# Two transformer blocks on one core: four first tiles instead of one go through the arriving token blocks

## The chip, the cores and the metric
The kernel runs on one core of a Trainium2 chip. The time is that of one launch in microseconds of device time. TensorE multiplies, VectorE (DVE), ScalarE (ACT) and GpSimd (POOL) work on rows of 128 partitions, SyncE (SP) issues all DMA transfers. Each engine runs its own instructions in order and waits at semaphores.

## The reference
Two blocks over 512 tokens of width 1024. Only the beginning matters here: the input norm, the first projection and the norm of the memory.

```python
h = rms_norm(x, norm_mix_g[layer])
proj = h @ w_in                                   # 2560 columns of the first mixer and 256 of q_mem
slab = token_shift(proj[..., :RWKV_COLS], mu)     # z + (z_prev - z) * mu
r, k, v, wd, ad, gd = split(slab)                 # 768 each; 64, 64, 128
log_w = -softplus(-(w0 + tanh(wd) @ w2)) - 0.5
a = sigmoid(a0 + ad @ a2);  g = sigmoid(gd) @ g2
kv = rms_norm(mem, mem_norm_g) @ w_mem_kv         # 256 memory tokens
```

The rest (a delta-rule scan over six pairs of heads, memory attention, two feed-forward parts, two kinds of local attention in the second block) is not touched.

## The kernel before, in words
The activations lie with the features in the partitions: eight blocks of 128 features by 512 tokens. (They are called token blocks here, as the functions that handle them are called `token`.) A weight unit is 128x1024. For precision every factor is split in a high and a low part (`Whi`, `Wlo`, `Hhi`, `Hlo`), and a block of a tile is three matmuls (hi·hi, lo·hi, hi·lo) of 128x512 into one PSUM bank (`mm3`, all at line 906). A tile is eight blocks, 24 matmuls. The norm's factor is applied behind the product, when the tile is evicted, so matmuls can run before the sum of squares is known.

`make_plan` writes one list of steps; each engine's program walks over it and emits its own share, so the order of the list is the order on every queue. `step` adds a step, `take` and `give` hand out buffers of a ring. Tiles are generators, one block per `next`, the eviction at their end. `unit` is called when a tile begins: it advances the splitting of weights (`splits`) to NW - 1 = 2 units ahead of the tile. A split of unit u is a cast on ScalarE (L1894) and a subtraction on VectorE (L1471); with three buffers it needs the tile of unit u - 3 ended. `splits(n)` also steps the loads up to unit u + 2; a load of unit u waits on SyncE's queue for the low part of unit u - 3.

At the front, each x block is loaded (L2283), multiplied with the gain to `Hhi` and squared on ScalarE (L1900, L1903), `Hlo` made by VectorE (L1477), and the squares added by GpSimd (L2178). Only tile wa (the lora columns) goes along. Then `around` runs gd, with the norm in it: `root` sums over the features by matmul, ScalarE takes the square root, VectorE the reciprocal, `rs` transposes it, RS is copied (L1514). The tiles slab (0,1), (0,0), (0,2) follow, and in them, by `weave`, `early`: the eight memory blocks (L1908, L1911 on ScalarE, L1482 on VectorE, L2184 on GpSimd), the decay and rate products (`sg`, `ta`), the scan (L1610) and the exponents (L2015). `early` alternates between the memory blocks and the others. Then `mem_projections` begins with root "m", which sums `accm`, the squares of the memory.

The eviction of a shift tile (wa, gd, slab) is: VectorE multiplies with RS (L1526), ScalarE copies with a factor (L1947), VectorE adds the shifted part (L1528) and only then goes on; ScalarE goes on to tanh for wa (L1951) and sigmoid for gd (L1954), each with a table load.

Of the kernel before, what the change touches and what calls it, by code (L numbers as in the profile page):

```python
# [9 lines left out]
ALU = mybir.AluOpType  # L10
ACT = mybir.ActivationFunctionType
# [15 lines left out]
NW = 3  # L27
# [24 lines left out]
def b_span(n):  # L52
    return max(0, n - 1), min(4, n + 2)
# [5 lines left out]
class Plan:  # L59
# [5 lines left out]
    def count(self, kind, *key):  # L65
        self.totals[kind] = self.totals.get(kind, 0) + 1
        self.numbers[(kind, *key)] = self.totals[kind]

    def step(self, kind, *key):
        self.steps.append((kind, *key))  # L70
        self.count(kind, *key)
# [37 lines left out]
def run(gen):  # L109
    for _ in gen:  # L110
        pass
# [28 lines left out]
def weave(main, filler, per):  # L140
    due = 0.0
    for weight in main:
        due += per * (weight or 1)
        while due >= 1:
            due -= 1
            next(filler, None)
# [21 lines left out]
def spaced(gen, took):  # L168
    for _ in gen:
        yield took  # L170


def make_plan(units):
    plan = Plan()
    step, count = plan.step, plan.count
# [3 lines left out]
    plan.X0 = x0 = Slots(4)  # L179
    plan.TB = tmps = Slots(4)  # L180
    plan.TC = late = Slots(4)
    state = {"loads": 0, "splits": 0, "units": 0, "lo": "wlo"}
    pend = []

    def flush():
# [9 lines left out]
    def splits(n):  # L195
        while state["splits"] < min(n, len(units)):
            u = state["splits"]
            loads(min(u + NW, len(units)))
            plan.numbers[("lo", u)] = state["lo"]
            step("split", u)  # L200
            count(state["lo"], u)
            state["splits"] += 1

    def unit(name):
        u = state["units"]
        assert units[u][0] == name, (units[u][0], name)
        state["units"] += 1
        splits(u + NW - 1)
        return u

    def bank(kind, *key):
# [85 lines left out]
    def norm(name):  # L297
        bank("root", *name)
        yield
        bank("rs", *name)  # L300

    def around(g1, g2, mid):
        for _ in range(8):
            next(g1)
        next(mid)
        for _ in range(3):
            next(g2)
        run(mid)
        run(g1)
        run(g2)  # L310


    for i in range(8):
        x0.take(("x", i))
        step("xload", i)
        if i < 2:
            loads(i + 1)
        if i == 3:
            step("cload")
        if i:  # L320
            ftmp.take(("x", i))
            ftmp.give(("x", i))
        step("x", i)
        count("Hlo", "x", i)
        x0.give(("x", i))
        if i == 0:
            splits(1)
    splits(2)
    step("memload")

    around(tile("wa", (18,), ("rw", 18), "x", range(8)), tile("gd", (19,), ("rw", 19), "x", range(8)),
           norm(("x",)))

    def mem_norm():
        for i in range(8):
# [48 lines left out]
    def projection(p, i):  # L384
        return couples(tile("slab", (p, i), ("rw", 6 * i + p), "x", range(8)))
# [100 lines left out]
        yield  # L486

    early = turns(normed, rates0())
    weave(itertools.chain(*(spaced(projection(0, i), 2) for i in (1, 0, 2))), early, 0.5)
    run(early)  # L490

    def front0():
# [60 lines left out]
    for u in range(4):  # L553
        w = unit(("va", u))
# [142 lines left out]
def block_program(nc, xT, memT, wts, vecs, cst, w2a2, g2, biasA, biasB, out, units):  # L697
    plan = make_plan(units)
# [18 lines left out]
    D, MB, OB = banks[0:2], banks[2:7], banks[7]  # L717
# [5 lines left out]
    Hhi1, Hlo = sb("Hhi", [128, 8, T], R), sb("Hlo", [128, 8, T], R)  # L723
# [4 lines left out]
    st8 = [sb(f"st8{i}", [128, 8])[:] for i in range(2)]  # L728

    arena = top[0]  # L730
    slab = [sb(f"slab{i}", [128, T]) for i in range(3)]
# [4 lines left out]
    sg, Pi, ta, kf, kn = (sb(n, [128, T]) for n in ("sg", "Pi", "ta", "kf", "kn"))  # L736
    Pp = sb("Pp", [128, NC, 65])
# [68 lines left out]
    def v(name, j=0):  # L806
        o, w = V_AT[name]
        return V[:, o + j:o + j + 1]
# [16 lines left out]
    def small(*root):  # L825
# [13 lines left out]
        "t1_out gv_out xu_out yu_out uw_out pd_out phi_out yo1_out st_out yo2_out mean_out tg_out "  # L839
        "ms_out mt_out va_act va_dve as_out at_out vbt_out "  # L840

        "setup zero dve wide xsq xadd msq madd hsq lora shift_a shift sgp tap cum kf0 exp pc kksq bt rk ar bb "
        "bk x0 y0 ai zsq tnv bonus mmax mrec pn hkb amax aexp arec an sqr gated gact gsig sig act resq "
        "sq_add").split()}

    def at_outs(n):

        return n + 1 + max(0, n - 15)

    def span(n):  # L850

        return (0, 2) if n < 16 else b_span(n % 4)

    def out_of(user):

        kind = user[0]
        if kind in ("rs", "hn", "kk", "tn"):
            return S["spread_out"], N("spread", *user)
        if kind == "va":
            j = user[1]  # L860
            return (S["va_dve"], j // 2 + 1) if j % 2 else (S["va_act"], j // 2 + 1)
        if kind == "mpv":
            return S["umem"], N("mpv_lo", *user[1:])
        if kind == "as":
            return S["as_out"], 2 * user[1] + user[2] + 1
        if kind == "at":
            return S["at_out"], at_outs(user[1] - 1) + user[2] + 1
        if kind == "odd":
            return S["Ulo"], N("Ulo", "att", 7)
        if kind in TWO:  # L870
            p, i = user[1:]
            return S[kind + "_out"], TWO[kind] * p + TWO[kind] - 1 + i
        return S[kind + "_out"], N(*user)
# [7 lines left out]
    evict_n = {}  # L881
# [20 lines left out]
    def tensor_program(e):  # L902
# [5 lines left out]
        def mm3(o, whi, wlo, xhi, xlo, first, last):  # L908
            mm(o, whi, xhi, first, False)
            mm(o, wlo, xhi, False, False)  # L910
            return mm(o, whi, xlo, False, last)
# [18 lines left out]

        def d_free(t):

            if t >= 2:
                if tiles[t - 2].kind == "vm":
                    w.wait_ge(S["vm_out"], tiles[t - 2].key[0] + 1)
                else:
                    w.wait_ge(S["evict"], evict_n[t - 2])

        def weight_block(t, i):
            x = tiles[t]  # L940
            hi, lo = acts(x.ver)
            if i == 0:
                w.wait_ge(*lo_of(x.unit))
                d_free(t)
            k, j, n = x.ks[i], x.cols[i], x.n
            whi, wlo = Wsp[x.unit % NW]
            written(x.ver, k)
            last = i == len(x.ks) - 1
            p = mm3(D[t % 2][:, 0:n], whi[:, j:j + 128], wlo[:, j:j + 128], hi[:, k, 0:n], lo[:, k, 0:n],
                    i == 0, last)  # L950
            if last:
                p.then_inc(S["tile"])
# [393 lines left out]
    def ftmp_of(user):  # L1346
        return ftmp[plan.F.at[user]]
# [94 lines left out]
    def vector_program(e):  # L1442
# [29 lines left out]
                                ALU.subtract).then_inc(S["wlo"])  # L1472

        def token(i):
            w.wait_ge(S["xsq"], i + 1)
            x = x0[plan.X0.at["x", i]][:]
            e.scalar_tensor_tensor(Hlo[:, i, :], x, v("gmix", i), Hhi1[:, i, :].bitcast(F), ALU.mult,  # L1477
                                   ALU.subtract).then_inc(S["Hlo"])

        def mem_token(i):  # L1480
            w.wait_ge(S["msq"], i + 1)
# [33 lines left out]

        def evict(t):
            x = tiles[t]
            b, n = D[t % 2], x.n
            w.wait_ge(S["tile"], tile_n[t])
            if x.kind in ("wa", "gd", "slab"):  # L1520
                j = 6 * x.key[1] + x.key[0] if x.kind == "slab" else x.key[0]
# [336 lines left out]
        def turn_vb(t):  # L1858
# [1 line left out]
            e.tensor_copy(vb[:], MB[plan.M.at["vbt", t]][:].rearrange("p (n x) -> p n x",  # L1860
                                                                     x=128)).then_inc(S["vbt_out"])

        steps = {"split": split, "x": token, "mx": mem_token, "root": root, "rs": norm_rows, "evict": evict,
                 "cum": cumulate, "kk": key_rows, "bo": bonus, "ops": operands, "xm": first_scores, "sb": score_b,
                 "sk": score_k, "t1": level_product, "xu": level_x, "yu": level_y, "pd": increments,
                 "phi": transfers, "st": state_step, "yo2": outputs_before, "mean": group_mean, "tn": group_rows, "tg": gate_rows,
# [19 lines left out]
    def scalar_program(e):  # L1886
# [9 lines left out]
        def token(i):  # L1896
            x = x0[plan.X0.at["x", i]][:]
            w.wait_ge(S["V"], 16)
            w.wait_ge(S[f"xin{i % 4}"], 16 * (i // 4 + 1))
            e.activation(Hhi1[:, i, :], x, ACT.Copy, scale=v("gmix", i))  # L1900
            if i:
                ftmp_free(w, ("x", i))
            e.activation((ftmp_of(("x", i)) if i else acc)[:], x, ACT.Square, scale=1.0).then_inc(S["xsq"])  # L1903
# [222 lines left out]
        def va_out():  # L2126
            w.wait_ge(S["va"], 4)
            w.wait_ge(S["wide"], N("root", "n", "gmix2"))
            for j in (0, 2):
                for o, lo, hi in va_parts(j):  # L2130
                    p = e.activation(o, MB[plan.M.at["va", j]][lo:hi, :], ACT.Copy, scale=rsnb[lo:hi, j:j + 1])
                p.then_inc(S["va_act"])

        steps = {"split": split, "x": token, "mx": mem_token, "root": root, "evict": evict, "sg": decay,
                 "ta": rate, "exps": exponents, "sq": key_square, "na": turned("na", lambda q: GA[q][:, :, 64:128], "yo1"),
                 "nb": turned("nb", lambda q: BR[q][:, :, 0:64], "phi", -1.0),
                 "vn": turned("vn", lambda q: Vn[q][:], "yo1"), "kn": turned("kn", lambda q: Kn[q][:], "pd"),
# [8 lines left out]
    def pool_program(e):  # L2146
# [3 lines left out]
        def turn():  # L2150

            if before[0]:
                w.wait_ge(*before[0])
# [3 lines left out]
        def done(instruction, sem):  # L2157
            counts[sem] = counts.get(sem, 0) + 1
            before[0] = (S[sem], counts[sem])
            instruction.then_inc(S[sem])  # L2160
# [5 lines left out]
        def split(u):  # L2166
            if plan.numbers[("lo", u)] == "wlo_pool":
# [2 lines left out]
                width, k = units[u][1], u % NW  # L2170
                done(e.tensor_tensor(Wsp[k][1][:, 0:width], Wraw[k][:, 0:width],  # L2171
                                     Wsp[k][0][:, 0:width].bitcast(F), ALU.subtract), "wlo_pool")

        def token(i):
            if i:
                w.wait_ge(S["xsq"], i + 1)
                turn()
                done(e.tensor_tensor(acc[:], acc[:], ftmp_of(("x", i))[:], ALU.add), "xadd")  # L2178

        def mem_token(i):  # L2180
            if i:
# [75 lines left out]
        def group_rows(p):  # L2257
# [1 line left out]
            turn()  # L2259
            done(e.tensor_tensor(y2, y2, bonus3[p % 3][:], ALU.add), "bonus")  # L2260

        steps = {"split": split, "x": token, "mx": mem_token, "evict": evict, "sg": decay, "ta": rate,
                 "exps": exponents, "kf": keys, "kk": key_rows, "ops": operands, "xm": first_scores,
                 "sb": score_b, "ai": states_from, "tn": group_rows}
        setup()
# [237 lines left out]
```

## Time and profile before

| | us |
|---|---|
| median of 3 runs (1604.68 to 1606.57) | 1606.14 |
| the profiled execution | 1605.55 |
| its span | 1603.8 |
| TensorE busy | 1535.5 (96%) |
| VectorE busy | 841.3 (52%) |
| ScalarE busy | 544.4 (34%) |
| GpSimd busy | 257.2 (16%) |

Of the chain of work that ended last 86% is TensorE's, 7% VectorE's, 3% ScalarE's. All that is changed lies in the first 60 us. Times are read from the span's start. The granted clock is given as a share of full speed; before its first record it is shown as 1.00, so at the very beginning the distance between matmuls tells it and not that column. Operations on an engine overlap a little: the distance between two starts can be shorter than the time of one.

### The profile page before, as it was taken

The page shows a single profiled execution, that of the slowest core. Times are in us where ns is not written, and L with a number is a line of the kernel's source. Part 1 is how long each engine was busy: PE and PEld are TensorE (multiplying, and loading weights), DVE is VectorE, ACT ScalarE, POOL GpSimd, SP SyncE. Part 2 cuts the span into 40 slices and gives each one's busy share as a digit, 9 for nine tenths or more (in the row PEclk, how much of TensorE's full clock was granted, in tenths as well). Part 3 has the DMA queues.
Part 4 walks back from the last instruction along what each step waited for, and adds up shares of the span by engine and source line. Part 5 has one row for each costly group of instructions (what it writes and reads, how often), then busy time and mean ns, then how long its engine had stood idle before and what let it go on. Part 6 is the DMA issues. An engine that isn't in the chain of part 4 may idle for free.

```text
span 1603.8 us, 26299 instructions
## 1 busy us (share of the span) xinstructions
PE 1535.5 (96%) x11198; PEld 1211.5 (76%) x11198; DVE 841.3 (52%) x1287; ACT 544.4 (34%) x871; POOL 257.2 (16%) x183
## 2 busy tenths in 40 slices
PE   6899999999789999999999999999989999999999
PEld 4666777777668888888878876676768888888887
DVE  6566466566445536353565446768565443443343
ACT  6443323332123213122244225655434232232131
POOL 3132233332011000000011001222222220120020
PEclk9999999999899999999999999999999999999999
DMA  6220000011012333323322323322133323333322
GB/s 213 66 67 15 28 28 28 28 41 68 3 53 92 100 88 100 97 89 105 92 92 80 97 67 105 92 89 63 53 91 92 93 92 106 92 93 105 87 88 102
DMA packets 38516, 127.65 MB, mean 80 GB/s; under 512 B 4224, under 2 KB 5248, under 8 KB 38400
## 3 DMA queue, kind: packets, MB, share of 16 engines
q1 hardware_dynamic: 38400, 125.97, 25.6%
q8 instruction: 89, 1.46, 0.4%
q14 instruction: 27, 0.22, 0.0%
HBM read 123.86 MB, written 2.10 MB: 79 GB/s over the span
## 4 chain that ended last, share of the span: by engine, by line
PE 86%; DVE 7%; ACT 3%; issue 2%; POOL 0%; DMA 0%; SPq 0%; POOLq 0%; ACTq 0%; DVEq 0%
PE bank L906 83%; PE bank L1285 1%; PE bank L1021 1%; DVE qa L1579 1%; DVE Hlo L1477 1%; DVE Wlo L1471 1%; ACT Whi L1894 1%; PE bank L1090 0%; DMA x<-in_xT 0%; DVE qa L1577 0%; PE bank L1243 0%; DVE ftmp L1526 0%; DVE Yi L1702 0%; ACT kbr L2094 0%; ACT Hhi L1969 0%
## 5 line engine op out<-in xcount | busy, mean ns | idle before, releaser
L906 PE MATMUL bank<-Hhi,Whi 128*128 128x512 f32 x912 | 377.5, 414 | 17.3 <-DVE Wlo L1471 10.2
L906 PE MATMUL bank<-Hhi,Wlo 128*128 128x512 f32 x912 | 362.9, 398 | 0.0
L906 PE MATMUL bank<-Hlo,Whi 128*128 128x512 f32 x912 | 360.3, 395 | 0.0
L906 PE MATMUL bank<-Uhi,Whi 128*128 128x512 f32 x736 | 291.7, 396 | 8.9 <-DVE Ulo L1748 4.0
L906 PE MATMUL bank<-Uhi,Wlo 128*128 128x512 f32 x736 | 287.8, 391 | 0.0
L906 PE MATMUL bank<-Ulo,Whi 128*128 128x512 f32 x736 | 287.6, 391 | 0.0
L1471 DVE TENSOR_TENSOR Wlo<-Wraw,Whi 128x1024 fp32r<-128x1024 f32 (+1 forms) x177 | 226.9, 1282 | 105.9 <-ACT Whi L1894 105.9
L1894 ACT CAST Whi<-Wraw 128x1024 fp32r<-128x1024 f32 (+1 forms) x216 | 223.3, 1037 | 161.9 <-PE bank L906 150.7
L906 PEld LDWEIGHTS bank<-Hhi,Whi 128*128 128x128 f32 x912 | 172.6, 189 | 75.9 <-issue 14.1
L906 PEld LDWEIGHTS bank<-Hlo,Whi 128*128 128x128 f32 x912 | 172.4, 189 | 42.4
L906 PEld LDWEIGHTS bank<-Hhi,Wlo 128*128 128x128 f32 x912 | 173.1, 190 | 33.2
L906 PEld LDWEIGHTS bank<-Uhi,Whi 128*128 128x128 f32 x736 | 138.8, 189 | 46.4 <-DVE Ulo L1748 4.8
L906 PEld LDWEIGHTS bank<-Ulo,Whi 128*128 128x128 f32 x736 | 138.7, 189 | 29.4
L906 PEld LDWEIGHTS bank<-Uhi,Wlo 128*128 128x128 f32 x736 | 138.9, 189 | 27.9 <-issue 0.2
L2171 POOL TENSOR_TENSOR Wlo<-Wraw,Whi 128x1024 fp32r<-128x1024 f32 x39 | 92.7, 2377 | 364.9 <-ACT Whi L1894 364.3
L1550 DVE TENSOR_TENSOR X<-X,bank 128x512 f32<-128x512 f32 x72 | 49.5, 687 | 171.5 <-PE bank L906 171.5
L2191 POOL TENSOR_TENSOR accb<-accb,tmpb 128x512 f32<-128x512 f32 x14 | 18.8, 1342 | 380.9 <-ACT tmpb L1993 380.9
L1963 ACT CAST Uhi<-tmpb 128x512 fp32r<-128x512 f32 x32 | 19.9, 621 | 148.7 <-DVE tmpb L1559 148.7
L2196 POOL TENSOR_TENSOR qa<-qa 128x512 f32<-128x512 f32 x22 | 28.5, 1293 | 198.3 <-ACT qa L1973 198.3
L1977 ACT CAST Hhi<-qa 128x512 fp32r<-128x512 f32 x22 | 13.7, 622 | 115.6 <-POOL qa L2201 115.6
L1557 DVE SCALAR_TENSOR_TENSOR tmpb<-bank,RSb 128x512 f32<-128x512 f32 x32 | 22.1, 691 | 45.5 <-PE bank L906 45.4
L2104 ACT ACTIVATE sr<-sr,st 128x256 f32<-128x256 f32 (+1 forms) x64 | 33.8, 528 | 34.1 <-DVE st L1823 18.3
(289 smaller groups left out, 1749.2 us busy)
## 6 DMA issues: line engine op xcount, KB each, us to landing
Wraw<-in_wts SPq DMA_DIRECT2D x208, 512.0 KB, 3.6
bA<-in_biasA SPq DMA_DIRECT2D x12, 256.0 KB, 2.6
Wraw<-in_wts SPq DMA_DIRECT2D x8, 384.0 KB, 3.1
x<-in_xT SPq DMA_DIRECT2D x8, 256.0 KB, 4.1
X<-in_xT SPq DMA_DIRECT2D x2, 1024.0 KB, 6.6
out<-X SPq DMA_DIRECT2D x8, 256.0 KB, 2.1
bB<-in_biasB SPq DMA_DIRECT2D x4, 384.0 KB, 3.2
memX<-in_memT SPq DMA_DIRECT2D x2, 512.0 KB, 7.2
```

Of the source, the lines that this page charges most:

```text
L906: return e.matmul(o, lhsT, rhs, start=start, stop=stop, skip_group_check=True)
L1021: p = e.transpose(b[:, 128 * j:128 * j + 128], sq[:, 128 * j:128 * j + 128], c("ident"))
L1285: p = e.transpose(o, sr[n % 3][:, x:x + 128], c("ident"))
L1471: e.tensor_tensor(Wsp[k][1][:, 0:width], Wraw[k][:, 0:width], Wsp[k][0][:, 0:width].bitcast(F), ALU.subtract).then_inc(S["wlo"])
L1550: e.tensor_tensor(y, y, z, ALU.add).then_inc(S["evict"])
L1557: e.scalar_tensor_tensor(z[:], b[:], 0.0, RSb[:], ALU.max, ALU.mult).then_inc(S["evict"])
L1894: e.copy(Wsp[u % NW][0][:, 0:width], Wraw[u % NW][:, 0:width]).then_inc(S["whi"])
L1963: e.copy(Uhi[:, x.key[1], :], tmp_of(("raw", t))[:]).then_inc(S["ffhi"])
L2104: p = e.activation(part, part, ACT.Exp, scale=1.0, bias=x[:, 2 + i:3 + i], accum_out=x[:, 4 + i:5 + i])
L2171: done(e.tensor_tensor(Wsp[k][1][:, 0:width], Wraw[k][:, 0:width], Wsp[k][0][:, 0:width].bitcast(F), ALU.subtract), "wlo_pool")
L2191: done(e.tensor_tensor(accb[:], accb[:], tmp_of(("sqr", *x.key))[:], ALU.add), "sq_add")
L2196: done(e.tensor_tensor(z[:], z[:], s[:], ALU.mult), "sig")
```

## The change
Tiles wa, gd and slab (0,1) now go through the token blocks together: wa from block 0, gd from block 1, slab (0,1) from block 2, each catching up when it enters. Slab (0,0) comes behind them, its first four blocks between root and rs of the norm. Tiles 2 and 3 get banks of the ring `MB`, and d_free no longer holds them back. Until all four are evicted, weights are split one unit ahead instead of two. The constants are loaded behind x5 instead of x3. `Hlo` waits for the high part alone, the squares are a step of their own (`xq`) behind the split, and VectorE adds them. ScalarE starts with a small copy that needs only GpSimd's memset. The remaining slab (0,2) has all of `early` woven in, at 1.5 for 0.5.

```diff
-    state = {"loads": 0, "splits": 0, "units": 0, "lo": "wlo"}
+    state = {"loads": 0, "splits": 0, "units": 0, "lo": "wlo", "ahead": 1}
...
-        splits(u + NW - 1)
+        splits(u + state["ahead"])
...
+    for t in (2, 3):
+        M.take(("first", t))
+    firsts = [tile(kind, key, ("rw", m), "x", range(8))
+              for kind, key, m in (("wa", (18,), 18), ("gd", (19,), 19), ("slab", (0, 1), 6))]
     for i in range(8):
         x0.take(("x", i))
         step("xload", i)
-        if i < 2:
+        if i < 3:
             loads(i + 1)
-        if i == 3:
+        if i == 5:
             step("cload")
+        step("x", i)
+        count("Hlo", "x", i)
+        if i < 3:
+            splits(i + 1)
         if i:
             ftmp.take(("x", i))
             ftmp.give(("x", i))
-        step("x", i)
-        count("Hlo", "x", i)
+        step("xq", i)
         x0.give(("x", i))
-        if i == 0:
-            splits(1)
-    splits(2)
+        for n, g in enumerate(firsts):
+            for _ in range(i + 1 if i == n else i > n):
+                next(g)
     step("memload")
-
-    around(tile("wa", (18,), ("rw", 18), "x", range(8)), tile("gd", (19,), ("rw", 19), "x", range(8)),
-           norm(("x",)))
+    firsts.append(tile("slab", (0, 0), ("rw", 0), "x", range(8)))
+    first_norm = norm(("x",))
+    next(first_norm)
+    for _ in range(4):
+        next(firsts[3])
+    run(first_norm)
+    for g in firsts:
+        run(g)
+    for t in (2, 3):
+        M.give(("first", t))
+    state["ahead"] = NW - 1
...
-    weave(itertools.chain(*(spaced(projection(0, i), 2) for i in (1, 0, 2))), early, 0.5)
+    weave(itertools.chain(*(spaced(projection(0, i), 2) for i in (2,))), early, 1.5)
...
+    def bank_of(t):
+        return MB[plan.M.at["first", t]] if t in (2, 3) else D[t % 2]
...
-            if t >= 2:
+            if t >= 4:
...
         def token(i):
-            w.wait_ge(S["xsq"], i + 1)
+            w.wait_ge(S["xhi"], i + 1)
...
+        def token_square(i):
+            if i:
+                w.wait_ge(S["xsq"], i + 1)
+                w.wait_ge(S["xadd"], i - 1)
+                e.tensor_tensor(acc[:], acc[:], ftmp_of(("x", i))[:], ALU.add).then_inc(S["xadd"])
...
-            e.activation(Hhi1[:, i, :], x, ACT.Copy, scale=v("gmix", i))
+            e.activation(Hhi1[:, i, :], x, ACT.Copy, scale=v("gmix", i)).then_inc(S["xhi"])
...
+        w.wait_ge(S["zero"], 1)
+        e.activation(st8[0], Pp[:, :, 0], ACT.Copy, scale=1.0)
```

GpSimd's `token` (L2174 to L2178) is removed.

## Rows read from the trace of the kernel before

**Rows 1.** Stretches: us, then busy us of PE, PEld, DVE, ACT, POOL; clock, DMA
```profile
8.72:23.77 15.05, 11.41 (x32) 6.54 (x33) 13.14 (x8) 10.69 (x16) 10.55 (x7) 1.00 0.83 289
...
53.44:58.70 5.26, 5.26 (x14) 4.32 (x15) 3.26 (x7) 3.82 (x5) 0.00 (x0) 0.50 0.09 36
```

**Rows 2.** Timeline of TensorE: start, us, operation, [idle before it, releaser]
```profile
16.00 0.63 PE L906 MATMUL bank<-Hhi,Wlo 128*128 128x512 f32 x1
...
16.43 0.63 PE L906 MATMUL bank<-Hlo,Whi 128*128 128x512 f32 x1
...
19.13 0.39 PE L906 MATMUL bank<-Hhi,Wlo 128*128 128x512 f32 x1
...
19.36 0.40 PE L906 MATMUL bank<-Hlo,Whi 128*128 128x512 f32 x1
...
22.99 1.05 PE L906 MATMUL bank<-C,acc 128*128 128x128 f32 x8
...
25.96 0.60 PE L1021 MATMUL bank<-C,acc 128*128 128x128 f32 x4
...
32.64 1.13 PE L906 MATMUL bank<-WA,w2s 64*128 64x512 f32 x4
...
43.29 0.50 PE L906 MATMUL bank<-Hhi,Whi 128*128 128x512 f32 x1 [1.12 <-DVE Wlo L1471]
...
53.44 1.22 PE L906 MATMUL bank<-C,accm 128*128 128x128 f32 x4 [4.38 <-POOL accm L2184]
```

**Rows 3.** Groups of instructions between 10 and 23 us, VectorE's low parts
```profile
L1477 DVE SCALAR_TENSOR_TENSOR Hlo<-x,V,Hhi 128x512 fp32r<-128x512 f32 x7 | 12.0, 1780 | 1.5 <-ACT ftmp L1903 1.5
```

**Rows 4.** Timeline of ScalarE, 0 to 80 us
```profile
3.94 1.28 ACT L1900 ACT_TABLE_LOAD   x1 [3.94 <-DMA x<-in_xT]
...
8.85 0.72 ACT L1900 ACTIVATE Hhi<-x,V 128x512 fp32r<-128x512 f32 x1 [1.44 <-DMA x<-in_xT]
...
24.24 1.04 ACT L1894 CAST Whi<-Wraw 128x1024 fp32r<-128x1024 f32 x1
...
28.15 0.72 ACT L1947 ACTIVATE WA<-ftmp,VD 128x512 f32<-128x512 f32 x1 [2.87 <-DVE ftmp L1526]
28.89 1.28 ACT L1951 ACT_TABLE_LOAD   x1
...
30.75 0.72 ACT L1947 ACTIVATE GD<-ftmp,VD 128x512 f32<-128x512 f32 x1
...
34.26 0.51 ACT L1908 ACTIVATE memHhi<-memX,V 128x256 fp32r<-128x256 f32 x1
...
34.98 0.67 ACT L1998 ACTIVATE sg<-bank,VD 128x512 f32<-128x512 f32 x1
...
44.00 0.63 ACT L2015 ACTIVATE Pp<-sg 128x512 f32<-128x512 f32 x1
```

**Rows 5.** Transfers issued at 1.63 and at 12.06 us: KB, us to landing
```profile
Wraw<-in_wts SPq DMA_DIRECT2D x1, 512.0 KB, 4.0
...
x<-in_xT SPq DMA_DIRECT2D x1, 256.0 KB, 2.5
```

**Rows 6.** Timeline of VectorE, 0 to 80 us
```profile
25.32 1.23 DVE L1471 TENSOR_TENSOR Wlo<-Wraw,Whi 128x1024 fp32r<-128x1024 f32 x1 [0.27 <-ACT Whi L1894]
...
27.42 0.69 DVE L1526 TENSOR_TENSOR ftmp<-bank,RS 128x512 f32<-128x512 f32 x1
28.91 0.75 DVE L1528 SCALAR_TENSOR_TENSOR WA<-ftmp,V,WA 128x511 f32<-128x511 f32 x1 [0.79 <-ACT WA L1947]
...
36.96 0.58 DVE L1482 SCALAR_TENSOR_TENSOR memHlo<-memX,V,memHhi 128x256 fp32r<-128x256 f32 x1 [0.95 <-ACT ftmp L1911]
37.46 1.77 DVE L1610 TENSOR_TENSOR_SCAN sg<-C,sg 128x512 f32<-128x512 f32 x1
```

**Rows 7.** Timeline of GpSimd, 0 to 80 us
```profile
45.06 1.30 POOL L2224 TENSOR_TENSOR kf<-kf,slab 128x512 f32<-128x512 f32 x1 [0.17 <-POOL PC L2218]
...
50.61 2.78 POOL L2184 TENSOR_TENSOR accm<-accm,ftmp 128x256 f32<-128x256 f32 x3 [2.49 <-ACT ftmp L1911]
```

More of the change, by code:

```diff
@@ L840, in block_program @@
         "ms_out mt_out va_act va_dve as_out at_out vbt_out "
-        "setup zero dve wide xsq xadd msq madd hsq lora shift_a shift sgp tap cum kf0 exp pc kksq bt rk ar bb "
+        "setup zero dve wide xhi xsq xadd msq madd hsq lora shift_a shift sgp tap cum kf0 exp pc kksq bt rk ar bb "
         "bk x0 y0 ai zsq tnv bonus mmax mrec pn hkb amax aexp arec an sqr gated gact gsig sig act resq "
@@ L867, in out_of @@
             return S["at_out"], at_outs(user[1] - 1) + user[2] + 1
+        if kind == "first":
+            return S["evict"], evict_n[user[1]]
         if kind == "odd":
@@ L948, in weight_block @@
             last = i == len(x.ks) - 1
-            p = mm3(D[t % 2][:, 0:n], whi[:, j:j + 128], wlo[:, j:j + 128], hi[:, k, 0:n], lo[:, k, 0:n],
+            p = mm3(bank_of(t)[:, 0:n], whi[:, j:j + 128], wlo[:, j:j + 128], hi[:, k, 0:n], lo[:, k, 0:n],
                     i == 0, last)
@@ L1517, in evict @@
             x = tiles[t]
-            b, n = D[t % 2], x.n
+            b, n = bank_of(t), x.n
             w.wait_ge(S["tile"], tile_n[t])
@@ L1861, in turn_vb @@
                                                                      x=128)).then_inc(S["vbt_out"])
-        steps = {"split": split, "x": token, "mx": mem_token, "root": root, "rs": norm_rows, "evict": evict,
+        steps = {"split": split, "x": token, "xq": token_square, "mx": mem_token, "root": root, "rs": norm_rows, "evict": evict,
                  "cum": cumulate, "kk": key_rows, "bo": bonus, "ops": operands, "xm": first_scores, "sb": score_b,
@@ L1899, in token, with token_square @@
             w.wait_ge(S[f"xin{i % 4}"], 16 * (i // 4 + 1))
-            e.activation(Hhi1[:, i, :], x, ACT.Copy, scale=v("gmix", i))
+            e.activation(Hhi1[:, i, :], x, ACT.Copy, scale=v("gmix", i)).then_inc(S["xhi"])
+        def token_square(i):
+            x = x0[plan.X0.at["x", i]][:]
             if i:
@@ L2132, in va_out @@
                 p.then_inc(S["va_act"])
-        steps = {"split": split, "x": token, "mx": mem_token, "root": root, "evict": evict, "sg": decay,
+        w.wait_ge(S["zero"], 1)
+        e.activation(st8[0], Pp[:, :, 0], ACT.Copy, scale=1.0)
+        steps = {"split": split, "x": token, "xq": token_square, "mx": mem_token, "root": root, "evict": evict, "sg": decay,
                  "ta": rate, "exps": exponents, "sq": key_square, "na": turned("na", lambda q: GA[q][:, :, 64:128], "yo1"),
@@ L2172, in split @@
                                      Wsp[k][0][:, 0:width].bitcast(F), ALU.subtract), "wlo_pool")
[L2174 to L2178, printed above, removed]
         def mem_token(i):
@@ L2260, in group_rows @@
             done(e.tensor_tensor(y2, y2, bonus3[p % 3][:], ALU.add), "bonus")
-        steps = {"split": split, "x": token, "mx": mem_token, "evict": evict, "sg": decay, "ta": rate,
+        steps = {"split": split, "mx": mem_token, "evict": evict, "sg": decay, "ta": rate,
                  "exps": exponents, "kf": keys, "kk": key_rows, "ops": operands, "xm": first_scores,
```

## The prediction

> **What bounds the kernel now.** I read the stretches first [rows 1]. Between the first matmul at 8.72 us and 23.77 us TensorE has only 32 records and is busy for 11.4 of 15.05 us, a good part of that at half speed: the starts lie 0.43 us apart at 16 us and 0.23 us apart at 19 us [rows 2], so the clock rose from its low level (1.2 GHz) to the high one (2.4) in between, nine microseconds after the first matmul. In this stretch it has one tile (24 matmuls) and waits for a token block at each step. VectorE's Hlo takes 1.78 us on average there [rows 3], beside GpSimd's additions.
>
> The timeline of TensorE shows two more stalls in front of the pair loop: 1.12 us at 43.29 for a split weight, and 4.38 us at 53.44, where the matmuls with `accm` wait for GpSimd's last addition [rows 2]. Behind the second the clock is at 0.50 until 58.70 [rows 1]. That second place is the one to watch. In TensorE's order the root of the memory norm stands right behind tile (0,2), and what it waits for is a chain over ScalarE, VectorE and GpSimd: four evictions with their table loads, weight splits, memory blocks. From root "x" (22.99) to it are 30.45 us. Whatever the change does ahead of 53.44 counts only by how it moves this point; behind it the plan is as before (the same splits made, the same steps due), so I carry the shift to the end unchanged.
>
> **Part 1, the start.** ScalarE's 1.28 us table load stands behind the arrival of x0 now [rows 4]; with a first activation that needs only a memset it is over before x0 lands. But what comes next is the cast of unit 0, and its weights land 4.0 us after their issue at 1.63 [rows 5], at 5.6. The cast of 24.24 leads its Wlo (25.32) by 1.08 us, and Wlo takes 1.23 [rows 4, 6]. First matmul at 8.0 instead of 8.72: 0.7 us, worth little, since x1 lands at 8.85 in any case [rows 4].
>
> **Part 2, the token blocks.** VectorE now adds the squares: 0.69 us each, taken from the tile's product (two operands of this size) [rows 6], at most the 1.78 of an Hlo beside GpSimd. With GpSimd quiet I take Hlo at the 0.75 us that the product of the same kind, WA's, takes [rows 6], so 1.44 us a block. On SyncE's queue, however, `splits(i + 1)` now puts the load of unit 3 ahead of x2 and that of unit 4 ahead of x3. The first waits for Wlo0 (8.0), the second for Wlo1 (x1 8.85, cast from 9.5, Wlo from 10.55, done 11.8). An unloaded x takes 2.5 us to land, a load 4.0 at the start [rows 5]. x2 then lands at 12.2 (between 10.9, if it passes the load, and 13), x3 at about 16.1, x4 and x5 within 1.3 us, x6 at 20.0 and x7 at 20.7. TensorE has three blocks a token from x3 on, 9 matmuls or 2.07 us at the high clock, so it hides these arrivals: nothing on the path, but x3 is within 1 us of being late.
>
> TensorE: 3 matmuls at 8.0, 3 at 10.4, then without a break from 11.8 (Wlo1). At 0.43 us until the clock rises, at 0.23 behind. Bounds of the rise: 13.3 (early, since it is busy without a break) and 17.7 (nine microseconds behind the first matmul as before). I take 15.0, nearer the early one, because from 11.8 nothing interrupts it. Then 6 + 3.2/0.43 = 13.5 matmuls are done, 58.5 are left, 13.5 us: root "x" starts at R = 28.5. The bounds give 27.7 and 29.8. Acc and the constants are there by 24.
>
> The Trainium skill has a rule against packing this stretch (TensorE: Matmul & The Clock Gate, Part 1): the low clock lasts for a time of sustained activity, not for a number of matmuls, so closer spacing means more of them at 1.2 GHz. By it the rise would be near the early bound, 13.3, and the sum 0.8 us lower; by this trace's nine microseconds it would be 1.3 higher. No row here shows TensorE busy without a break at the low clock so early.
>
> At R three tiles are done; before, gd and slab (0,1) were 48 matmuls from 23.77, 11.0 us, with sg, ta and the transposes (1.1 and 0.6) between, so to about 36.4 [rows 1, 2]. Here sg, ta, root and transposes, some 2.5 us, are yet to come. TensorE is 5 to 6 us ahead here. The question is what is late next.
>
> **Part 3, the fourth tile and its split.** `ahead` is 1 until all four evictions are in the plan. So the split of unit 3 stands behind root "x": cast behind the square root, Wlo behind the reciprocal. Before, Wlo started 2.33 us after the root's matmuls (22.99 to 25.32) [rows 2, 6]; the same here, done at R + 3.6, where before TensorE had gd's weights ready. Stall 2.5 us. Four blocks: R + 6.4. The transposes follow, and from their start to the first product it was 1.46 us before (25.96 to 27.42), so R + 7.8 [rows 2, 6]. TensorE does its last four blocks to R + 9.8 and then needs unit 4.
>
> **Part 4, four evictions in a row.** Each is product, ScalarE copy 0.73 behind, VectorE's second product 0.76 behind that, next product 0.8 further: 2.3 us [rows 4, 6]. WA adds tanh and GD sigmoid, each with a table load, so the next copy starts 2.6 us behind (28.15 to 30.75) [rows 4]. Copies therefore start at R + 8.5 (WA), 11.1 (GD; it waits for tanh), 13.7 (slab 1; sigmoid) and, by the 2.3 again, 16.0 (slab 0). Only behind that stand the cast of unit 4 (R + 16.65) and its Wlo (17.7 to 18.9). TensorE idles from R + 9.8 to R + 18.9: 9.1 us with nothing to do, R = 28.5 making it 47.4. Before, tile (0,2) started at 43.29 with its 1.12 us stall [rows 2]. All of the lead is lost here and 4.1 us more. In the kernel before these evictions lay beside gd's and slab's matmuls, with two units split ahead.
>
> **Part 5, tile (0,2) and the memory norm.** Idle of 4.38 us put the clock at 0.50 for 5.26 us [rows 1, 2]; 9.1 us will too. Six matmuls at 0.43: R + 21.5. Then sg and ta, 1.13 us for their four at the high clock [rows 2], about 1.9 here: R + 23.4. ScalarE's two tanh and memory block 1 (a block takes 0.72, 34.26 to 34.98) [rows 4]: R + 24.8. VectorE's memHlo (0.5, 36.96 to 37.46) and scan 1.77 [rows 6]: R + 27.0. Exp; GpSimd's kf starts 1.06 us behind it (44.00 to 45.06) and takes 1.30 [rows 4, 7]: R + 29.4. Behind it stand five additions, since `early` alternates and 1.5 steps a weight put all in one tile: 2.78/3 = 0.93 each [rows 7], 4.6 us: R + 34.0. TensorE is through at R + 28 and waits for these.
>
> **The sum.** 28.5 + 34.0 = 62.5 against 53.44: +9.1 us. The profiled execution took 1605.55 us (span 1603.8), so 1614.6; the median of the runs is 0.6 above it: 1615. Ends: R 27.7 to 29.8, and on the 34.0 the scan at 1.3 instead of 1.77 and additions at 0.8 (-1.1), the clock not falling (-1.8), contention or one more wait (+1.5). That is 1611.5 to 1618.
>
> **The rivals.** (a) The lead is kept. If Wlo4 were made beside tile (0,0), tile (0,2) would start at R + 9.8 and the chain of part 5 without the low clock (34.0 - 18.9 - 1.8) would take 13.3 us: root "m" at 51.6, -1.8 us, 1604.3; with R at its early 27.7, 1603.5. It decides as soon as the cast of unit 4 doesn't stand behind slab 0's copy on ScalarE. For it: ScalarE is busy only half of this time. Against: the step order puts it there, and engines run in order. To gain over 0.2% it would need another microsecond, as by a high clock from 12 us on. Chance 0.08, half of it below -0.2%.
> (b) Nothing is gained or lost to speak of: R comes at 25.5 (clock high from 12 on, no break) and the clock holds over the idle time (-1.8), the scan takes 1.3 (-0.5): 31.7 behind R, 57.2, +3.8; with a little more overlap within 0.2%. For it: the low clock at the start is not in the record of the granted clock. Against: [rows 2]. 1609.9; chance 0.12.
> (c) The token blocks become the bound: x2 and x3 later than worked out because the loads' waits on SyncE add up, TensorE dry for 2 to 3 us and its clock low for longer: R about 31, 1617.5. For it: the 1 us of slack of x3. Chance 0.15.
> (d) The change doesn't bring three tiles side by side (a bank or a wait orders them): part of the 72 matmuls is left for the time behind x7; R about 31 too. 0.03.
>
> **How the numbers follow.** Forecast 0.62, (a) 0.08, (b) 0.12, (c) and (d) 0.18. 0.2% is 3.2 us, about what can be told from no change. Faster: half of (a) and a little for shifts behind the front, whose place in the clock's turns changes: 0.07. Same: the other half of (a) and a third of (b), 0.08. Slower 0.85. The range leaves out (a) and the far ends of (b) and (c): 1609 to 1618.5.
>
> **What would show it.** In the changed profile: the first matmul near 8.0; Hlo at 0.75; x3's block later than 15.5; root "x" at 27.7 to 29.8; a TensorE wait of about 9 us for Wlo ahead of tile (0,2), at about 47, with the cast right behind the copy of slab 0; a clock of 0.50 behind it; GpSimd's accm releasing the root near 62. Wrong: if tile (0,2) starts before 43, or the accm wait is gone, or the shift at the memory root isn't the shift of the end (some later wait takes it up).

## The result and the profile after

The changed kernel takes 1616.03 us in the median (1615.25 to 1618.25, 4 runs) against 1605.58 for the kernel before: ratio 1.0067, 95% interval 1.0054 to 1.0079. It is 10.45 us slower; 1615 was forecast. Its profiled execution took 1618.25 us, the slowest of the four, with a span of 1616.5, so the traces differ by 12.7 us, some 2 more than the medians. No other execution of it has a trace.

First, the timeline of TensorE in the changed kernel (start, us, operation, idle before it and its releaser), at the places that answer to [rows 2].

```profile
8.05 0.80 PE L927 MATMUL bank<-Hhi,Whi 128*128 128x512 f32 x1 [8.05 <-DVE Wlo L1492]
...
11.02 0.80 PE L927 MATMUL bank<-Hhi,Whi 128*128 128x512 f32 x1 [1.32 <-DVE Hlo L1498]
...
16.86 0.57 PE L927 MATMUL bank<-Hhi,Wlo 128*128 128x512 f32 x1
17.27 0.39 PE L927 MATMUL bank<-Hlo,Whi 128*128 128x512 f32 x1
...
29.77 1.05 PE L927 MATMUL bank<-C,acc 128*128 128x128 f32 x8
33.37 0.50 PE L927 MATMUL bank<-Hhi,Whi 128*128 128x512 f32 x1 [2.55 <-DVE Wlo L1492]
...
37.82 0.60 PE L1042 MATMUL bank<-C,acc 128*128 128x128 f32 x4
...
50.19 0.80 PE L927 MATMUL bank<-Hhi,Whi 128*128 128x512 f32 x1 [9.02 <-DVE Wlo L1492]
...
53.05 1.97 PE L927 MATMUL bank<-WA,w2s 64*128 64x512 f32 x4
...
65.98 1.22 PE L927 MATMUL bank<-C,accm 128*128 128x128 f32 x4 [6.65 <-POOL accm L2211]
```

From 11.02 to 29.77 there is no wait: the token blocks are filled, as intended. Then come three stalls, 2.55, 9.02 and 6.65 us. The memory root stands at 65.98 instead of 53.44, 12.5 us later, and the span ends 12.7 us later: what happened ahead of this point is the whole change.

ScalarE's timeline shows what stands ahead of the cast of unit 4 (it answers to [rows 4]):

```profile
31.03 1.03 ACT L1921 CAST Whi<-Wraw 128x1024 fp32r<-128x1024 f32 x1
39.98 0.72 ACT L1977 ACTIVATE WA<-ftmp,VD 128x512 f32<-128x512 f32 x1 [7.92 <-DVE ftmp L1553]
...
42.55 0.70 ACT L1977 ACTIVATE GD<-ftmp,VD 128x512 f32<-128x512 f32 x1
...
45.10 0.71 ACT L1977 ACTIVATE slab<-ftmp,VD 128x512 f32<-128x512 f32 x1
47.23 0.72 ACT L1977 ACTIVATE slab<-ftmp,VD 128x512 f32<-128x512 f32 x1 [1.42 <-DVE ftmp L1553]
47.86 1.97 ACT L1921 CAST Whi<-Wraw 128x1024 fp32r<-128x1024 f32 x2
```

Four copies stand there, with two table loads among them, and behind the fourth the casts (x2: of units 4 and 5). ScalarE had been idle for 7.92 us ahead of the first. VectorE's and GpSimd's rows close the chain:

```profile
39.26 0.69 DVE L1553 TENSOR_TENSOR ftmp<-bank,RS 128x512 f32<-128x512 f32 x1
...
48.92 2.36 DVE L1492 TENSOR_TENSOR Wlo<-Wraw,Whi 128x1024 fp32r<-128x1024 f32 x2 [0.18 <-ACT Whi L1921]
```
```profile
61.73 4.20 POOL L2211 TENSOR_TENSOR accm<-accm,ftmp 128x256 f32<-128x256 f32 x5
```

The stretches give the clock (columns as in [rows 1]): 12 matmuls of slab (0,0), the idle time, tile (0,2)'s beginning, and what follows the memory root.

```profile
33.37:37.82 4.45, 4.45 (x12) 3.44 (x13) 0.00 (x0) 0.00 (x0) 0.00 (x0) 0.62 0.42 118
40.79:50.19 9.40, 0.39 (x2) 0.00 (x0) 6.03 (x9) 7.94 (x11) 0.00 (x0) 0.70 0.00 0
50.19:54.95 4.76, 4.76 (x10) 2.35 (x10) 1.48 (x2) 0.36 (x2) 0.00 (x0) 0.52 0.70 213
...
65.98:71.70 5.72, 5.72 (x16) 4.66 (x17) 2.52 (x5) 3.82 (x5) 0.00 (x0) 0.50 0.06 10
```

### The profile page after: what moved, and what is told of

It reads as the page before. It is cut to its first block, busy times and chain, and to the rows that moved or that the text cites. A ratio compares the mean times of both kernels' runs of the same rounds, so it can differ in the third digit from the quotient of the medians.

```text
span 1616.5 us, 26295 instructions
## 1 busy us (share of the span) xinstructions
PE 1539.1 (95%) x11198; PEld 1216.2 (75%) x11198; DVE 837.6 (52%) x1294; ACT 545.0 (34%) x872; POOL 246.5 (15%) x176
## 4 chain that ended last, share of the span: by engine, by line
PE 87%; DVE 7%; ACT 3%; issue 2%; POOL 1%; DMA 0%; SPq 0%; POOLq 0%; ACTq 0%; DVEq 0%
PE bank L927 84%; PE bank L1306 1%; PE bank L1042 1%; DVE qa L1606 1%; DVE Wlo L1492 1%; ACT Whi L1921 1%; PE bank L1111 0%; DMA x<-in_xT 0%; DVE qa L1604 0%; PE bank L1264 0%; DVE Yi L1729 0%; ACT kbr L2124 0%; DVE ftmp L1553 0%; ACT Hhi L1999 0%; DVE T L1719 0%
## 5 line engine op out<-in xcount | busy, mean ns | idle before, releaser
L2223 POOL TENSOR_TENSOR qa<-qa 128x512 f32<-128x512 f32 x22 | 28.5, 1294 | 198.3 <-ACT qa L2003 198.3
```

Of the source, the lines that this page charges most:

```text
L2223: done(e.tensor_tensor(z[:], z[:], s[:], ALU.mult), "sig")
```

## The experiments

The theory was that the order of the steps costs the time: unit 4's split, and then the memory blocks, stand behind four evictions. Its rival was that the token stage costs it: x2 and x3 behind weight loads, matmuls at the low clock, root x late. The ratios are to the kernel before, on the same chip. Kernels that ran on different chips are compared by these ratios. The three places (start of root x, of tile (0,2) and of the memory root, in us) are read from one profiled execution of each kernel.

| | ratio | 95% interval | root x | tile (0,2) | memory root |
|---|---|---|---|---|---|
| before | 1 | | 22.99 | 43.29 | 53.44 |
| changed | 1.0067 | 1.0054 to 1.0079 | 29.77 | 50.19 | 65.98 |
| e1 splits ahead | 1.0040 | 1.0028 to 1.0053 | 29.68 | 46.76 | 62.15 |
| e2 memory early | 1.0022 | 1.0012 to 1.0031 | 28.86 | 50.68 | 59.76 |
| e4 x before weights | 1.0065 | 1.0052 to 1.0078 | 29.65 | 50.08 | 65.77 |
| e5 squares on GpSimd | 1.0058 | 1.0046 to 1.0070 | 29.05 | 49.51 | 64.84 |
| e6 all moved | 1.0004 | 0.9995 to 1.0012 | 29.36 | 40.96 | 51.07 |
| e11 and exponents late | 0.9968 | 0.9956 to 0.9981 | 29.56 | 41.30 | 49.81 |
| e3 before, squares on VectorE | 0.9974 | 0.9963 to 0.9986 | 19.97 | 40.45 | 50.60 |
| e9 and memory sooner | 0.9958 | 0.9945 to 0.9970 | 19.57 | 42.55 | 49.75 |
| e10 and table load | 0.9952 | 0.9938 to 0.9965 | 19.83 | 42.81 | 50.01 |
| e12 memory spread | 0.9969 | 0.9957 to 0.9981 | 21.04 | 41.58 | 48.05 |

**e1: the splits ahead of the evictions.**

```diff
     run(first_norm)
+    splits(6)
     for g in firsts:
```

> The changed kernel with units 3 to 5 split ahead of the four evictions (one line: splits(6) between rs and the evictions). Theory (the order of the steps): what is lost stands in the queue behind the four evictions. Then TensorE's 9.0 us wait for unit 4 shrinks to about 3.9 us (it then waits for the product of slab (0,1)'s eviction, at 44.7), scalar work starts on the memory blocks behind the last copy (47.9), and the root of the memory norm comes at about 59.3 instead of 65.98: 6 to 7 us faster than the changed kernel, 1609 to 1610. Rival (the token blocks: low clock, late x2 and x3): the root of the first norm at 29.8 decides, and the time stays 1616.

Measured 1612.74 us, some 4 below the changed kernel by the ratios, in place of 6 to 7. The direction is the theory's, the size is not. TensorE and VectorE of e1 show why it is less:

```profile
46.76 0.77 PE L928 MATMUL bank<-Hhi,Whi 128*128 128x512 f32 x1 [5.68 <-DVE ftmp L1554]
...
62.15 1.22 PE L928 MATMUL bank<-C,accm 128*128 128x128 f32 x4 [6.64 <-POOL accm L2212]
```
```profile
38.96 2.35 DVE L1493 TENSOR_TENSOR Wlo<-Wraw,Whi 128x1024 fp32r<-128x1024 f32 x2
41.23 0.68 DVE L1554 TENSOR_TENSOR ftmp<-bank,RS 128x512 f32<-128x512 f32 x1
```

The wait of 9.02 us is 5.68 now, and another holds it: the bank, freed by slab (0,1)'s product. But the two splits stand ahead of the first product on VectorE, and put it from 39.26 to 41.23. I had moved the splits past the evictions at no price; the price is these 2.0 us on everything behind. The wait for accm stays as it was, 6.64 us.

**e2: the memory blocks ahead of the evictions.** `run(mem_norm())` in front of `run(first_norm)`, and `early = rates0()` alone.

> The changed kernel with only the eight memory blocks moved, from tile (0,2) to the place ahead of the four evictions, where ScalarE and VectorE are idle. Theory: the root of the memory norm no longer waits for GpSimd and follows tile (0,2) directly; that tile still starts at 50 to 51.5 behind the late split of unit 4, so the root comes at about 60.5 instead of 65.98, and the low clock behind it is gone: 7 to 9 us faster, 1607 to 1609. Rival (token blocks): no change, 1616. Rival (one chain, not two): if the two stalls are the same ScalarE work counted twice, only 1 to 3 us.

Measured 1609.68 us, 7 below the changed kernel by the ratios (0.0045 x 1606): the gain is the expected one, at its lower end. Its TensorE:

```profile
32.46 0.50 PE L927 MATMUL bank<-Hhi,Whi 128*128 128x512 f32 x1 [2.55 <-DVE Wlo L1492]
...
35.32 0.60 PE L1042 MATMUL bank<-C,acc 128*128 128x128 f32 x4
...
50.68 0.79 PE L927 MATMUL bank<-Hhi,Whi 128*128 128x512 f32 x1 [12.00 <-DVE Wlo L1492]
...
59.76 0.60 PE L927 MATMUL bank<-C,accm 128*128 128x128 f32 x4
```

Tile (0,2) starts no sooner, its wait is even longer (12.0 us), but the root has no wait at all. So the memory blocks are a cost of their own, not one chain counted twice.

**e3: one part of the change alone, in the kernel before.** `xq` as a step of its own, the additions on VectorE, `Hlo` waiting for `xhi`.

> The kernel before with one part of the change alone: squares added by VectorE, Hlo waiting for the high part only. Theory: Hlo falls from 1.78 to 0.75 us, x7's Hlo is done near 18 instead of 22, root x and all behind it come 3 to 4.5 us sooner: 1601 to 1603. Rival (arrival of the x blocks or the low clock sets their rhythm): under 1 us, 1605 to 1606.

Measured 1602.28 us, as expected, and the whole interval of the ratio lies below 1. (e7 is the same kernel again, run once on the same chip: 1603.44.) VectorE's groups from 10 to 20 us:

```profile
L1478 DVE SCALAR_TENSOR_TENSOR Hlo<-x,V,Hhi 128x512 fp32r<-128x512 f32 x7 | 5.2, 747 | 2.0 <-ACT Hhi L1907 1.8
L1485 DVE TENSOR_TENSOR acc<-acc,ftmp 128x512 f32<-128x512 f32 x7 | 4.8, 684 | 0.0
```

0.75 us for Hlo against 1.78 [rows 3]: root x comes 3.0 us sooner and all behind it by some 2.8. The edit has two sides, the adder and the earlier signal for Hlo, and they were not run apart. But in the kernel before VectorE makes the seven Hlo in a row without idle time (12.0 us for them [rows 3]), so what shortens the row is that each is shorter. Of the parts of the change that were tried with one tile (this one, and the table load in e10) it is the one that pays.

**e4: x2 and x3 issued before the weight loads of units 3 and 4.** In the loop `xload` 1, 2 and 3 are stepped together at i = 1.

> The changed kernel with x2 and x3 issued right behind x1, ahead of the loads of units 3 and 4 (the order of the kernel before). Theory: the late arrivals are hidden, since TensorE has matmuls from 11 us on without a break; root x moves by under 0.5 us and the time stays within 1 us of 1616. Rival (token blocks): 2 to 4 us faster.

Measured 1617.83 us, ratio 1.0065 against 1.0067: no difference that can be told. ScalarE takes up x3 at 13.68 instead of 16.59, and root x is still at 29.65 instead of 29.77. The late arrivals are hidden, and this half of the rival falls.

**e5: the squares on GpSimd again, in the changed kernel.** `xq` on GpSimd, as `token` was.

> The changed kernel with the squares added by GpSimd again (the order of everything else kept). Theory: VectorE's pace is hidden here. With 1.8 us an Hlo the x blocks still come faster than TensorE's 2.07 us a token, so root x stays within 0.7 us of 29.8 and the time within 1 us of 1616. Rival (the moved additions cost VectorE, or bring, what is seen): 2 us or more to either side.

Measured 1616.39 us, ratio 1.0058 against 1.0067: not to be told apart. The same part that brings 4 us in e3 brings nothing here, since TensorE, and not VectorE, sets the pace of the tokens with three tiles: in e5 too it has no wait from 11.04 to root x. Groups of e5, 8 to 29 us:

```profile
L2208 POOL TENSOR_TENSOR acc<-acc,ftmp 128x512 f32<-128x512 f32 x7 | 11.1, 1582 | 14.4 <-ACT ftmp L1930 14.0
...
L1498 DVE SCALAR_TENSOR_TENSOR Hlo<-x,V,Hhi 128x512 fp32r<-128x512 f32 x7 | 7.6, 1082 | 7.1 <-ACT Hhi L1924 7.0
```

**e6: everything moved.** The changed kernel with

```diff
-    first_norm = norm(("x",))
+    first_norm, normed = norm(("x",)), mem_norm()
+    for _ in range(4):
+        next(normed)
     next(first_norm)
     for _ in range(4):
         next(firsts[3])
+    run(normed)
     run(first_norm)
+    splits(5)
...
-    early = turns(normed, rates0())
-    weave(itertools.chain(*(spaced(projection(0, i), 2) for i in (2,))), early, 1.5)
+    early = rates0()
+    weave(itertools.chain(*(spaced(projection(0, i), 2) for i in (2,))), early, 0.34)
...
-            if t >= 4:
+            if t in (4, 5):
+                w.wait_ge(S["evict"], evict_n[t - 4])
+            elif t >= 6:
```

> The changed kernel with unit 4 split ahead of the evictions, four memory blocks ahead of root x and four behind it, tiles 4 and 5 waiting only for the eviction that last used their bank (tiles 0 and 1), sg and ta after the fourth block of tile (0,2). Theory: with both queues cleared three tiles side by side pay at last: tile (0,2) starts at about 41, the root of the memory norm at about 48 against 53.44 in the kernel before, with no low clock behind it; 6 to 8 us faster than before, 1598 to 1600. Rival (the token blocks cost what they bring): root x at 29.8 is 7 us later than before and the time is 1605 or above.

Measured 1606.77 us, ratio 1.0004: 10 us below the changed kernel by the ratios, but no gain over the kernel before. My 6 to 8 us were wrong, the rival's "1605 or above" is what came, though not for its reason alone. TensorE of e6:

```profile
46.62 0.50 PE L930 MATMUL bank<-Hhi,Whi 128*128 128x512 f32 x1
...
47.23 0.63 PE L930 MATMUL bank<-Hlo,Whi 128*128 128x512 f32 x1
...
50.60 0.40 PE L930 MATMUL bank<-Hhi,Wlo 128*128 128x512 f32 x1
...
51.07 0.61 PE L930 MATMUL bank<-C,accm 128*128 128x128 f32 x4
...
59.92 0.41 PE L1047 MATMUL bank<-C,accm 128*128 128x128 f32 x2 [2.79 <-DVE rsn L1538]
...
61.41 0.80 PE L930 MATMUL bank<-Hhi,Whi 128*128 128x512 f32 x1 [1.07 <-DVE Wlo L1497]
```

Tile (0,2) starts at 40.96, as expected (41), but the root comes at 51.07, not 48. The three us lie inside this tile: sg and ta take 2.77 us of TensorE's time (43.85 to 46.62, a wait of 0.59 in it) where the kernel before needs 1.06, and the clock is low from 47.23 to 50.60, so that the last 12 matmuls take 4.45 us and not 2.85 as in e11. Behind the root are two new waits, where the kernel before has none. ScalarE's rows name the cause of these: exponents and their table load stand ahead of the memory root's square root, and the cast of unit 6 behind that.

```profile
55.14 1.28 ACT L2050 ACT_TABLE_LOAD   x1
...
57.60 1.28 ACT L1961 ACT_TABLE_LOAD   x1
...
59.06 1.03 ACT L1926 CAST Whi<-Wraw 128x1024 fp32r<-128x1024 f32 x1
```

**e11: e6 with the exponents behind the memory root.** `step("exps", 0)` and `step("kf", 0)` at the head of `front0`.

> The kernel of e6 with the exponents and kf moved behind the root of the memory norm. Theory: e6 lost 2.8 us there to the transposes waiting for VectorE and 1.1 us to the split of unit 6, both behind two table loads and the exponents on ScalarE. They go: 2 to 4 us below e6, 1603 to 1605, and still not below e3, because root x at 29.4 stays late. Rival: e6's stall comes from the table load of the square root itself and only moves: within 1 us of e6's 1606.8.

Measured 1601.88 us, ratio 0.9968: 5 to 6 us below e6 by the ratios, more than expected. The transposes wait for 0.62 us instead of 2.79:

```profile
49.81 0.60 PE L930 MATMUL bank<-C,accm 128*128 128x128 f32 x4
...
57.79 0.41 PE L1047 MATMUL bank<-C,accm 128*128 128x128 f32 x2 [0.62 <-DVE rsn L1538]
```

Not all of this is the order. In these two traces 1.3 us are gained at the root already, where e11 has no low clock ahead of it, and e6's clock is also low from 62.00 to 67.55, behind its waits, where e11's is not.

So a kernel with three tiles side by side can be faster than the kernel before, with the order mended. This is where the rival (token blocks) ends: root x is as late here (29.56) as in the changed kernel, and the kernel is 16 us faster than it by the ratios. That the three tiles themselves bring something is not shown: e11 is not to be told from e3 (0.9968 and 0.9974), which has one tile and the squares on VectorE.

**e9, e10, e12: the same queue in the kernel before.** There too TensorE waits 4.38 us for accm [rows 2]. e9 takes e3 and steps the memory blocks two at a time in tile (0,1), the rest after them.

> The kernel before with the squares on VectorE (as in e3) and the eight memory blocks woven in two at a time in tile (0,1), decay, rate, scan and exponents after them. Theory: the 4.4 us wait for accm ahead of the memory root, and the low clock of about 5 us behind it, are the same queue that costs in the changed kernel; without it the memory root follows tile (0,2) directly, near 46 instead of 50.6: 4 to 7 us below e3's 1602, 1596 to 1598. Rival (ScalarE is full there, and the wait moves to a weight split): within 1 us of 1602.

Measured 1600.87 us, ratio 0.9958 (e3: 0.9974): a gain of 2 to 3 us, less than the 4 to 7, and the intervals of the two overlap, so that the gain itself is not certain. Both sides had a part. TensorE and VectorE of e9:

```profile
42.55 0.50 PE L914 MATMUL bank<-Hhi,Whi 128*128 128x512 f32 x1 [3.13 <-DVE Wlo L1479]
...
44.21 0.63 PE L914 MATMUL bank<-Hhi,Whi 128*128 128x512 f32 x1
...
49.75 0.60 PE L914 MATMUL bank<-C,accm 128*128 128x128 f32 x4
```
```profile
32.28 6.67 DVE L1496 SCALAR_TENSOR_TENSOR memHlo<-memX,V,memHhi 128x256 fp32r<-128x256 f32 x8
38.87 0.68 DVE L1540 TENSOR_TENSOR ftmp<-bank,RS 128x512 f32<-128x512 f32 x1
```

The wait for accm (4.42 us in e3) is gone; 2.0 us of it came back as a longer wait for unit 4's split, and 1.5 as a low clock behind that wait (44.21 to 47.20), which tile (0,2) in e3 doesn't have. A denser weave of all of `early` in e3 (1.0 for 0.5, e8) has no time: its steps wait for each other in a circle, a deadlock.

> The kernel of e9 with ScalarE's small first copy (the table load off x0's path). Theory: first matmul near 8.0 instead of 8.7, but x1 lands at 8.9 to 9.8 in any case and sets everything behind: under 0.7 us faster than e9, not to be told from it. Rival: the 1.28 us of the load come back in full, 1.3 us faster than e9.

Measured 1600.07 us, ratio 0.9952. First matmul at 8.09 for 8.67, root x at 19.83 for 19.57: the table load off the path brings nothing that can be told, as expected. It has the lowest ratio here and is faster than both kernels; e9 is not to be told from it.

> The kernel of e9 with the eight memory blocks less dense: five in tile (0,1), three in tile (0,0) between decay, scan and exponents. In e9 eight memHlo in a row held VectorE until 38.95, so the product of tile (0,1)'s eviction came at 38.87, its copy at 39.58, the cast of unit 4 behind it, and TensorE waited 3.1 us at 42.55. Theory: that wait shrinks to 1 us or less (1.1 in the kernel before) and the memory root still finds its sum ready: 1.5 to 3 us faster than e9, 1598 to 1599. Rival: the wait for accm comes back at the memory root (its last block is later) and eats the gain: 1600 to 1602.

Measured 1600.94 us, ratio 0.9969: not faster than e9, the rival's side. The wait ahead of (0,2) did shrink, to 0.47 us, but two others came:

```profile
41.58 0.50 PE L916 MATMUL bank<-Hhi,Whi 128*128 128x512 f32 x1 [0.47 <-DVE Wlo L1481]
...
48.05 0.71 PE L916 MATMUL bank<-C,accm 128*128 128x128 f32 x4 [0.69 <-POOL accm L2197]
...
51.02 0.80 PE L916 MATMUL bank<-Hhi,Whi 128*128 128x512 f32 x1 [2.25 <-DVE Wlo L1481]
```

## Why the prediction was right

**Start.** First matmul at 8.0 forecast, 8.05 measured. By e10 it is worth nothing that can be told.

**Token blocks.** No break from x1 on, as forecast, and root x at 29.77 within its bounds (27.7 to 29.8), 1.3 us later than the 28.5 taken. Some 1.1 us of this is the rise of the clock, at 17.27 and not 15.0; x1 was late too, taken up by ScalarE at 9.46 and not 8.85. That nine microseconds after the first matmul came true in this trace (9.2) is luck and no rule. In the other profiled kernels the rise came 5.7 to 9.0 us after the first matmul (at 14.50 in e3, 14.74 in e2, 16.9 in e4), and with three tiles root x started between 28.86 and 29.77: later than the 28.5 taken in all seven of them. The early bound, 13.3, was worked out from no row, and no rise here is as early.

The Trainium skill (TensorE: Matmul & The Clock Gate, Part 1) says that the low clock lasts for a time and not for a number of matmuls, and by it I had weighed the early end. The two traces agree as far as they go: 17 matmuls began at the low clock in 9.2 us here, 14 in 9.0 us in the kernel before.

The late blocks are hidden, x6 too, which ScalarE took up at 22.57 and not 20.0: for x2 and x3 e4 shows it. That the square's engine doesn't matter here is shown by e5.

**The fourth tile.** The stall for unit 3 was to be 2.5 us, to R + 3.6: it is 2.55, to 29.77 + 3.60. What I left out is the clock: it fell behind this stall, and 12 matmuls took 4.45 us instead of 2.8. The first product stands at R + 9.5, not 7.8. In e2, with the same stall of 2.55 us, it did not fall: the 12 matmuls took 2.86 us (32.46 to 35.32). But it did in e1, e4 and e5, with this stall, and in e6 and e11, with 2.90 and 3.05 us. So the term belongs in the sum, at up to 1.7 us.

**Four evictions.** Copies were to start 2.6, 2.6 and 2.3 us apart; they are 2.57, 2.55 and 2.13 apart. The cast follows at once, idle time 9.0 us (9.1 forecast). e1 moves the cast and the idle time shrinks to 5.7: shown.

**Memory norm.** From tile (0,2) to the root 15.1 us forecast, 15.8 measured, GpSimd releasing it, the clock low at the start of the tile and again behind the root. sg and ta took 1.97 us (1.9). e2 takes this chain away and 7 us with it: shown.

**The sum.** R + 34.0 forecast, R + 36.2 measured; +9.1 forecast, +12.5 in this trace, +10.45 in the medians. R + 36.2 is above the range's upper end (R + 35.5): the clock in the fourth tile (+1.7) and the memory norm (+0.7) make it so. That the median lies within 1 us of the 1615 forecast is therefore in part luck. This execution was the slowest of the four, and no trace shows whether the clock fell behind the stall in the others. The rest behind the root is the same in both, as the two shifts (12.5 and 12.7) show.

**The rivals.** (a), the lead kept: its condition, that the cast is not behind slab (0,0)'s copy, is what e1 sets up, and its 1604 did not come (1612.74), since the freed bank and the memory chain follow; it needed e6 and e11. (c), the token blocks as bound, is excluded by e4 and by the unbroken row from 11.02; only its longer low clock came, within the bounds. (b) wanted root x at 25.5, and it stood at 29.77. (d) did not happen: all 72 matmuls of the three tiles stand ahead of root x.

What stays open: what decides whether the clock falls behind a stall of 2.5 us, and what three tiles side by side are worth by themselves, with all else in the best order.

## What to carry to other kernels

Filling an idle engine moves the work of the others: ask what now stands between the end of the filled stretch and the next thing that the first engine needs, in queue order. Here three tiles done early meant four evictions in a row, and what stood behind them (a split, a bank, the memory blocks) cost more than the filling brought. And compare with the cheap end: one tile with a faster VectorE (e9) reaches the memory root at 49.75, three tiles side by side in the best order tried (e11) at 49.81.

## What was not expected of the hardware

- The clock fell after 2.55 us of idle time and 1.05 us of 128x128 matmuls in front of it (starts 0.43 us apart from 34.48 on), in four of the five profiled kernels with this stall; in the fifth (e2) it did not. In e6 it fell again from 47.23 to 50.60, behind sg and ta and a wait of only 0.59 us, and in e11, with the same steps and a wait of 0.55 us, it did not. What decides it, no run shows.
- VectorE's two-input product takes 0.75 us alone, 1.78 beside GpSimd's additions, but only 1.08 on average when the tokens are spread wider and the two meet less (e5: 0.75 for the three in which GpSimd adds nothing, 1.1 to 1.5 for the others), though a GpSimd addition is no shorter, 1.58 on average for 1.51.
